# Twenty weight tiles of a two-block kernel: x^T and its remainder as one 512-column operand, sums made by VectorE

## The reference, cut to what matters

```
u = x @ w_in_conv                 # layer 0: query of the cross-attention (256 columns) and 3 x 768 columns
tok = conv(b * c) * c0            # "conv", parts 1, 2 and 0 of u
u = x @ w_in_mlstm                # layer 1: queries and keys of the four heads, 2 x 768 columns
q, k = silu(depthwise_conv4(u_q)), silu(depthwise_conv4(u_k))
a, gate = split(x @ w_in_2[:, 512:1536])
z = a * sigmoid(gate)             # GLU, then a depthwise convolution of 31 taps
```

## Time and profile before

| | |
|---|---|
| median of 3 runs | 1468.51 us (1465.85 to 1469.38) |
| the profiled execution, its own time | 1467.67 us |
| its span, first to last instruction | 1465.9 us |
| PE (TensorE matmul) busy | 1431.2 us, 98% |
| VectorE / ScalarE busy | 905.6 us, 62% / 697.5 us, 48% |
| mean granted clock of TensorE | 0.99 |
| the chain that ended last, PE's share | 88% |

### The profile page before, as it was taken

One profiled execution on the slowest core, in us unless ns is written; L12 is line 12 of the kernel. 1 busy time (PEld: TensorE's weight loads), 2 busy tenths in 40 slices (PEclk: granted clock), 3 DMA queues, 4 the chain that ended last, 5 costly groups with the idle time before them and its releaser, 6 DMA issues.

```text
span 1465.9 us, 21137 instructions
## 1 busy us (share of the span) xinstructions
PE 1431.2 (98%) x8624; PEld 1176.9 (80%) x8624; DVE 905.6 (62%) x1477; ACT 697.5 (48%) x1145; POOL 51.7 (4%) x116
## 2 busy tenths in 40 slices
PE   8999999999999999999999999998999999999995
PEld 7888899888888988889898888888899996445431
DVE  7666577666676765667768666668888685121122
ACT  7455554454554644545755545445546553112211
POOL 0000000000000000000022000001000040000000
PEclk9999999999999999999999999999999999999997
DMA  9754554565555555444345655543554479999996
GB/s 347 282 192 175 199 201 144 201 230 175 199 182 191 202 197 205 173 163 168 131 151 208 251 186 187 200 163 137 181 177 143 144 307 373 391 421 421 421 421 267
DMA packets 49623, 333.80 MB, mean 228 GB/s; under 512 B 5744, under 2 KB 6000, under 8 KB 11632
## 3 DMA queue, kind: packets, MB, share of 16 engines
q1 hardware_dynamic: 47792, 321.50, 58.7%
q10 hardware_dynamic: 1728, 10.88, 1.9%
HBM read 331.31 MB, written 1.05 MB: 227 GB/s over the span
## 4 chain that ended last, share of the span: by engine, by line
PE 88%; DVE 4%; DMA 3%; ACT 2%; POOL 2%; issue 1%; DVEq 0%; SPq 0%; POOLq 0%; ACTq 0%
PE psw L601 55%; PE psy L601 31%; PE psw L604 2%; DMA raw<-in_we 2%; DVE wlo L1912 1%; DMA hold<-in_we 1%; ACT whi L1358 0%; POOL r L2765 0%; DVE x L1997 0%; DVE xs L1921 0%; DVE x L2010 0%; DMA ar<-in_xT 0%; ACT gb L1471 0%; DVE r L1979 0%; POOL rstd L2723 0%
## 5 line engine op out<-in xcount | busy, mean ns | idle before, releaser
L601 PE MATMUL psw<-xs,whi 128*128 128x512 f32 (+1 forms) x2384 | 652.8, 347 | 6.7 <-DVE wlo L1912 6.6
L1912 DVE TENSOR_TENSOR wlo<-raw,whi 128x1024 fp32r<-128x1024 f32 (+4 forms) x415 | 477.0, 1193 | 82.9 <-ACT whi L1358 78.1
L601 PE MATMUL psw<-xs,wlo 128*128 128x256 f32 x1848 | 489.5, 281 | 0.0
L601 PEld LDWEIGHTS psw<-xs,whi 128*128 128x128 f32 x2384 | 404.5, 190 | 54.3 <-DVE wlo L1912 6.6
L1358 ACT ACTIVATE whi<-raw 128x1024 fp32r<-128x1024 f32 (+4 forms) x415 | 402.2, 1024 | 8.7 <-PE psy L601 6.6
L601 PEld LDWEIGHTS psw<-xs,wlo 128*128 128x128 f32 x1848 | 350.4, 190 | 15.2 <-DVE wlo L1912 0.2
L1358 ACT ACTIVATE hf<-psw 128x256 f32<-128x256 f32 x82 | 30.9, 383 | 203.3 <-PE psw L601 203.3
L1950 DVE TENSOR_TENSOR hf<-hf,psw 128x256 f32<-128x256 f32 x82 | 34.0, 419 | 146.3 <-ACT hf L1358 146.3
L1358 ACT ACTIVATE ar<-psw 128x256 f32<-128x256 f32 (+3 forms) x125 | 55.0, 443 | 128.2 <-PE psw L601 115.8
L601 PE MATMUL psy<-whi,hhi 128*128 128x512 f32 x352 | 111.2, 390 | 0.0
L601 PE MATMUL psy<-whi,hlo 128*128 128x512 f32 x352 | 111.0, 389 | 0.0
(11 more groups left out here) (341 smaller groups left out, 1752.2 us busy)
## 6 DMA issues: line engine op xcount, KB each, us to landing
raw<-in_ws SPq DMA_DIRECT2D x189, 1024.0 KB, 4.8
hold<-in_we SPq DMA_DIRECT2D x46, 1024.0 KB, 12.5
raw<-in_we SPq DMA_DIRECT2D x24, 1024.0 KB, 12.9
ar<-in_we SPq DMA_DIRECT2D x21, 1024.0 KB, 13.3
gb<-in_ln ACTq DMA_DIRECT2D x8, 1024.0 KB, 5.0
raw<-in_ws SPq DMA_DIRECT2D x9, 768.0 KB, 4.1
raw<-in_ws SPq DMA_DIRECT2D x4, 672.0 KB, 3.8
raw<-in_ws SPq DMA_DIRECT2D x8, 256.0 KB, 6.7
```

The source lines that it names most:

```text
L601: return e.matmul(o, l, rr, start=start, stop=stop)
L1912: e.tensor_tensor(wlo[i % NS][:, c0:c1], raw_t[slot[i]][:, c0:c1], whi[i % NS][:, c0:c1].bitcast(f32), ALU.subtract).then_inc(*made.up((i, ...
```

## The change

The 20 tiles go through `parted` instead of `pair`. Each now takes two banks. ScalarE copies columns 256 to 511 of each bank to SBUF (`second_halves`), VectorE adds columns 0 to 255 there and thereby empties the bank (`summed`). What read a bank before now reads the sum in SBUF: `cz` is `cb * c2`, `cacc` is multiplied by `c0`, tap 3 and the other taps are made from `zp`, the sigmoid from `sg`, and the GLU's product takes `sg0`. `c2` and `c0` are new tiles in SBUF; the score matmuls of layer 0 wait for VectorE's sum and not for ScalarE's copy.

```
-        cb = arena.take(2 * T)
+        cb, c2, c0 = [blocks(arena.take(2 * T), 256) for _ in range(3)]
...
-        sg = hfl[:, 0:512]
+        sg, sg0 = hfl[:, 0:512], hfl[:, 512:1024]
... tensor
-                need.wait_ge(*act.at("query", l))
+                need.wait_ge(*(act.at("query", 1) if l else dve.at("summed", "q", 0, 1)))
...
-                pair(("q", 0), Tile("w_in_conv", 2304), xhi, xlo, x_rows(1))
+                parted(("q", 0), Tile("w_in_conv", 2304), x_rows(1))
...
-                        pair(("conv", part, j), Tile("w_in_conv", 768 * part + 256 * j), xhi, xlo, x_rows(1))
+                        parted(("conv", part, j), Tile("w_in_conv", 768 * part + 256 * j), x_rows(1))
...
-                        pair(("head", j, part), Tile("w_in_mlstm", 768 * part + 256 * j), xhi, xlo, x_rows(4))
+                        parted(("head", j, part), Tile("w_in_mlstm", 768 * part + 256 * j), x_rows(4))
...
-                pair(("glu", 0, j), Tile("w_in_2", 512 + 256 * j), xhi, xlo, x_rows(6))
+                parted(("glu", 0, j), Tile("w_in_2", 512 + 256 * j), x_rows(6))
... scalar
+            def second_halves(o, *key):
+                for j in range(2):
+                    need.wait_ge(*pe.at("bank", (*key, j)))
+                    copy(o[:, j, :], place[(*key, j)][:, 256:512]).then_inc(*act.up(("half", *key, j)))
... scalar, conv_mixer
-                    from_bank(("conv", 1, j), cb, flat, ("cb", j))
+                    second_halves(cb, "conv", 1, j)
                     steps.pop(0)()
                     w.tile()
+                    second_halves(c2, "conv", 2, j)
                     steps.pop(0)()
                     w.tile()
+                    second_halves(c0, "conv", 0, j)
... scalar, head
-                    copy(zp[part][:, :, 3:259], blocks(b[:, :], 256)).then_inc(*act.up(("zp", j, part)))
+                    second_halves(zp[part][:, :, 3:259], "head", j, part)
...
-                        ins = copy(q_[:, f, :], b[:, 256 * f:256 * f + 256], scale=qwt[:, blk, 3:4])
+                        need.wait_ge(*dve.at("summed", "head", j, part, f))
+                        copy(q_[:, f, :], zp[part][:, f, 3:259], scale=qwt[:, blk, 3:4]).then_inc(*act.up(("tap3", j, part, f)))
... scalar, glu
                 w.tile()
+                need.wait_ge(*(dve.at("zc", 0) if j else act.at("squares", 1, 1)))
+                second_halves(blocks(sg0, 256), "glu", 0, j)
                 between()
                 w.tile()
-                e.activation(sg, place["glu", 1, j][:, :], ACT.Sigmoid).then_inc(*act.up(("sg", j), took(("glu", 1, j))))
+                second_halves(blocks(sg, 256), "glu", 1, j)
+                need.wait_ge(*dve.at("summed", "glu", 1, j, 1))
+                e.activation(sg, sg, ACT.Sigmoid).then_inc(*act.up(("sg", j)))
... vector
+            def summed(o, *key):
+                for j in range(2):
+                    need.wait_ge(*act.at("half", *key, j))
+                    e.tensor_tensor(o[:, j, :], o[:, j, :], place[(*key, j)][:, 0:256], ALU.add).then_inc(
+                        *dve.up(("summed", *key, j), took((*key, j))))
... vector, conv_mixer
                     w.tile()
-                    need.wait_ge(*act.at("cb", j))
-                    need.wait_ge(*pe.at("bank", ("conv", 2, j)))
-                    then(e.tensor_tensor(cz[q][:, :, 2:258], blocks(cb, 256), blocks(place["conv", 2, j][:, :], 256), ALU.mult),
-                         took(("conv", 2, j)))
+                    summed(c2, "conv", 2, j)
+                    need.wait_ge(*dve.at("summed", "conv", 2, j, 1))
+                    then(e.tensor_tensor(cz[q][:, :, 2:258], cb, c2, ALU.mult))
... vector, head
                     need.wait_ge(*pool.at("zp", part))
+                    summed(zp[part][:, :, 3:259], "head", j, part)
... vector, GLU: the sums stand right behind w.tile()
             w.tile()
+            summed(blocks(sg, 256), "glu", 1, 0)
             glu(0)
             w.tile()
+            summed(blocks(sg0, 256), "glu", 0, 1)
             conv_some(5)
             w.tile()
+            summed(blocks(sg, 256), "glu", 1, 1)
             conv_some(5)
```

More of the change, by code:

```diff
@@ L967, in glu @@
             def glu(j, between=lambda: None):
-                pair(("glu", 0, j), Tile("w_in_2", 512 + 256 * j), xhi, xlo, x_rows(6))
+                parted(("glu", 0, j), Tile("w_in_2", 512 + 256 * j), x_rows(6))
                 between()
-                pair(("glu", 1, j), Tile("w_in_2", 1024 + 256 * j), xhi, xlo, x_rows(6))
+                parted(("glu", 1, j), Tile("w_in_2", 1024 + 256 * j), x_rows(6))
             def latents_turned():
@@ L1464, in query @@
                 w.tile()
-                from_bank(("q", l), mem_of[l].qT.rearrange("p b n -> p (b n)"), flat, ("query", l))
+                if l:
+                    from_bank(("q", l), mem_of[l].qT.rearrange("p b n -> p (b n)"), flat, ("query", l))
+                else:
+                    second_halves(mem_of[l].qT, "q", l)
             def score(l, h):
@@ L1522, in head @@
                 def head(j, part):
-                    b = place["head", j, part]
                     q_ = qk[j % 2][part]
-                    need.wait_ge(*pe.at("bank", ("head", j, part)))
                     if j:
                         need.wait_ge(*dve.at("taps", j - 1, part))
-                    copy(zp[part][:, :, 3:259], blocks(b[:, :], 256)).then_inc(*act.up(("zp", j, part)))
+                    second_halves(zp[part][:, :, 3:259], "head", j, part)
                     if j > 1:
@@ L1533, in head @@
                         blk = 6 * part + 2 * j + f
-                        ins = copy(q_[:, f, :], b[:, 256 * f:256 * f + 256], scale=qwt[:, blk, 3:4])
-                        ins.then_inc(*act.up(("tap3", j, part, f), *([took(("head", j, part))] if f else [])))
+                        need.wait_ge(*dve.at("summed", "head", j, part, f))
+                        copy(q_[:, f, :], zp[part][:, f, 3:259], scale=qwt[:, blk, 3:4]).then_inc(*act.up(("tap3", j, part, f)))
                 def head_silu(j, part):
@@ L2107, in conv_mixer @@
                     w.tile()
+                    summed(cb, "conv", 1, j)
                     steps.pop(0)()
                     w.tile()
-                    need.wait_ge(*act.at("cb", j))
-                    need.wait_ge(*pe.at("bank", ("conv", 2, j)))
-                    then(e.tensor_tensor(cz[q][:, :, 2:258], blocks(cb, 256), blocks(place["conv", 2, j][:, :], 256), ALU.mult),
-                         took(("conv", 2, j)))
+                    summed(c2, "conv", 2, j)
+                    need.wait_ge(*dve.at("summed", "conv", 2, j, 1))
+                    then(e.tensor_tensor(cz[q][:, :, 2:258], cb, c2, ALU.mult))
                     steps.pop(0)()
@@ L2126, in conv_mixer @@
                     w.tile()
-                    need.wait_ge(*dve.at("cacc", j, 1))
-                    need.wait_ge(*pe.at("bank", ("conv", 0, j)))
-                    e.tensor_tensor(cacc[q], cacc[q], blocks(place["conv", 0, j][:, :], 256),
-                                    ALU.mult).then_inc(*dve.up(("gated", j), took(("conv", 0, j))))
+                    summed(c0, "conv", 0, j)
+                    need.wait_ge(*dve.at("summed", "conv", 0, j, 1))
+                    e.tensor_tensor(cacc[q], cacc[q], c0, ALU.mult).then_inc(*dve.up(("gated", j)))
                     steps.pop(0)()
@@ L2301, in glu @@
                 need.wait_ge(*act.at("sg", j))
-                need.wait_ge(*pe.at("bank", ("glu", 0, j)))
+                need.wait_ge(*dve.at("summed", "glu", 0, j, 1))
                 need.wait_ge(*pool.at("zc"))
-                e.tensor_tensor(zc[:, 2 * j:2 * j + 2, 30:286], blocks(sg, 256), blocks(place["glu", 0, j][:, :], 256),
-                                ALU.mult).then_inc(*dve.up(("zc", j), took(("glu", 0, j))))
+                e.tensor_tensor(zc[:, 2 * j:2 * j + 2, 30:286], blocks(sg, 256), blocks(sg0, 256), ALU.mult).then_inc(*dve.up(("zc", j)))
             w.tile()
+            summed(blocks(sg0, 256), "glu", 0, 0)
             for n, blks in enumerate(LATENT_BANKS):
@@ L2731, in gpsimd @@
                 rstd_of(1, t)
-            need.wait_ge(*act.at("query", 0))
+            need.wait_ge(*act.at("half", "q", 0, 1))
             for q in range(2):
```

4 lines of the change are left out of this document (1 added, 3 removed).

## The result

The changed kernel takes 1470.38 us (median of 20 runs, 1468.66 to 1471.51) against 1467.32 us for the kernel before beside it (20 runs): a ratio of 1.0019, interval 1.0013 to 1.0025. By that ratio it is 2.8 us more (the medians themselves lie 3.06 us apart), where the forecast had 1.0 us less. The time lies inside the range and inside 0.3%, but it is clear of no change, and on the other side of it. The profiled span grew from 1465.9 to 1469.4 us. In a later round one execution of 2877.62 us (fifth_b) and one of 1773.76 us (the kernel before) are slow ones, left out of the ratios.

What follows compares the result with a forecast made beforehand. It took TensorE to bound the kernel (busy 1431 of 1466 us). Convolution -1.6, head stage +1.2 and GLU -0.64 gave -1.0 us, so 1467.5 us on the median (chance 0.57), range 1464.0 to 1471.5 us.

Steps and rivals of the forecast that it cites:

- The tile: Each of 20 tiles: 32 matmuls in 5.59 us instead of 48 in 5.75, 0.16 us gained, 3.2 us in all.
- Convolution stage: Ten tiles, no wait of PE for a bank, 1.6 us gained.
- The margins: Convolution stage: VectorE's sums empty banks 0.3 and 0.5 us before PE wants them; if both fail, 1 us is given back.
- GLU stage: Four tiles, no wait, 0.64 us gained; first product into `zc` about 1.6 us later.
- Head stage: Six tiles: 0.96 us gained, 1.3 + 0.8 + 0.1 us lost, so 1.2 us slower.
- The two waits for sums: Head stage: PE waits for banks 1.3 us at tile (1,0)'s second half and 0.8 us at (1,1)'s start.
- Attention 2: End of the head stage: two adds lengthen the last tile's copy, taps and SiLU by 0.1 to 0.3 us; costed at 0.1.
- The gain: Head stage: six tiles, each 0.16 us shorter on TensorE, 0.96 us in all.
- A: Rival: no wait in the head stage, as VectorE and ScalarE are further ahead; -3.2 us, 1465.3 us; chance 0.20.
- D: Rival: new tiles miss the feed-forward's pace, nothing gained, the waits stay; +2.2 us, 1470.7 us; chance 0.04.
- C: Rival: ScalarE's and VectorE's chain paces the head stage, 1.3 us at each of six tiles; +4.6 us, 1473.1 us; chance 0.07.
- B: Rival: each of two head-stage waits brings a fall of TensorE's clock, 1.67 us each; +2.3 us, 1470.8 us; chance 0.12.

Runs made afterwards that it cites:

- fifth_b: Changed kernel with the second halves of head tiles (1,0) and (2,0) in the fifth bank, 7, instead of the rotation of four; ratio to the kernel before 1.0014.
- heads_only: Kernel before with only the six head tiles on the new form; ratio to the kernel before 1.0033.
- after_again: The changed kernel run once more, nothing altered, for a second profile; ratio to the kernel before 1.0017.
- taps_first: Changed kernel with ScalarE's and VectorE's next-weight work moved behind each head tile's copies, sums and taps (last tile: behind its SiLU too); ratio to the kernel before 1.0000.
- tap_dve: Changed kernel with the heads' tap 3 made by VectorE from the sum instead of by ScalarE; ratio to the kernel before 1.0014.
- tap_again: Second run, for another profile, of the changed kernel with the heads' tap 3 on VectorE; ratio to the kernel before 1.0014.

## Why the prediction was wrong, by its own steps

**The tile: right.** 32 matmuls and 5.59 to 5.60 us; 8304 matmuls in all.

**Convolution stage: right.** -1.51, -1.65, -1.75 and -1.78 us where -1.6 was forecast, with no wait. The margins held as walked: VectorE's second remainder ends at 233.6 us, and the same stretch begins 0.46 us later than in the kernel before, so that this is 233.1 us against the forecast 233.0 to 233.3; the sum follows at once.

**GLU stage: right.** -0.64 to -0.69 us, forecast -0.64; the first product into `zc` begins 8.01 us after the start of the stage's second tile (1024.27 us in the chain) in place of 6.43 (1020.16), 1.6 us later as said.

**Head stage: the step that failed.** The term of the sum that was mis-sized is its +1.2 us: the two profiles of the changed kernel give +4.5 and +3.3, heads_only +2.95. The two waits for sums were right. The losses at the two ends of the stage were put at 0.1 us, the gain of 0.96 us was taken in full, and a further fall of the clock was left to a rival. In its parts:
- The two waits for banks were walked rightly, 1.42 and 0.91 us against 1.3 and 0.8, at the places named.
- The decay weights' wait was not looked at. It was 0.24 us before, and grew to 0.59 with the new convolution (TensorE comes 0.35 us earlier), 0.43 with the new head tiles (0.19), 0.80 with both (0.56): what TensorE gains ahead of it is waited away, as ScalarE's copies of v come when they come. So 0.4 us of the convolution's gain never reached the stage.
- Attention 2 was costed at 0.1 us "to 0.3" and took 0.64 more. The walk added two sums to the chain from tile to SiLU, and left out that they stand behind VectorE's remainder (until 757.96 us in the changed kernel, 0.9 us after the tile's end) and that ScalarE waits 0.70 us for them; 4.8 us became 5.4.
- The gain was 0.62 us in the stage, not 0.96 (after_again): tile (1,0) with its wait taken off is 0.1 us longer than before. Besides, a gap of 0.4 us more lies ahead of (2,0).
- One additional fall of the clock in one of the two profiles. Tile (1,1) takes 1.56 us more by it, the stage 1.2 us, as the gap ahead of (2,0) goes.

Together, for after_again: 1.4 + 0.9 + 0.55 + 0.63 + 0.4 + 0.1 for a slower attention 0 - 0.62 = 3.3 us, the measured difference.

**The rivals.** A is out, and so is D, as the tiles run at 5.59 us. C had the mechanism that the runs bore out, that the chain of ScalarE and VectorE sets the stage's length: fifth_b showed it by moving the waits, and taps_first by removing them. It was priced at 7.8 us by charging each of six tiles, and given 0.07; the small matmuls of the stage hold it to 2 to 3 us. Its condition, ScalarE's round with the waits in it, was met for a time: the roundings in the changed kernel begin at 722.83, 730.22 and 737.66 us, 7.4 us apart, although ScalarE is busy for only two thirds of the stage. In the first of these rounds 2.9 us are waits for VectorE (1.27 and 1.66 us). What counts is the time from a tile's end to its last sum and its SiLU. B had the price of a fall right (1.67 us, now 1.7), and its 1470.8 us, like D's 1470.7, lies next to the measured 1470.38. For D that is luck, for B in part: B has a fall behind each of the two waits, and the first profile shows one behind the second wait, the second profile none. B alone is not what made the kernel slower, as after_again and heads_only have 3.5 to 4 us of waits and one fall, as many as the kernel before; but the further fall is a part of the loss in the first profile.

Over whole executions the granted clock is 0.990 in the changed kernel (median of 31) and 0.992 in the kernel before (median of 110), some 2.9 us of clock more lost. It is no price: it takes in the end of the span, where the profiles lose 3.4 to 6.9 us from 1425 to 1455 us, and the kernels with the new convolution and GLU alone have 0.991 and are not slower. It leans towards further falls in the executions without a profile, and does not settle it.

The Trainium skill ("TensorE: Matmul & The Clock Gate", section A second HAM failure mode: psum-queue depth-cycling) names short idling between bank groups as what makes the clock swing. The count of falls leans that way, two against one on the mean, and so does their place behind waits; but tap_dve has two falls with no wait for a bank, and the same waits come with and without a fall. Why the one execution has more of them than the other is open.

**The sum.** Its sign hung on one term: three terms of -1.6, +1.2 and -0.6 us, of which the second was 2.1 to 3.3 us too small. With +3.3 in its place the three come to +1.0 us, which turns the sign but is not the measured +2.8. The first profile has the remainder in the further fall and in 0.5 us between 800 and 1016 us, the second in 1.7 us behind 1210 us. Which of these a usual execution has is not shown.

## What to carry to other kernels

When the emptying of a bank goes from one engine to two, walk the whole way from a tile's end to the release and to the tile's last consumer, with everything that stands in line on both queues, and put the copy, the sum and what follows ahead of the work for later tiles; here that order alone took the ratio from 1.0019 to 1.0000 (with what it changed in waits and falls of the clock together), and a further bank gave nothing that can be told from the error (1.0014). A gain ahead of a wait is worth only the part that the wait doesn't take back, so list the small waits too (0.2 us can become 0.8). A wait that covers another (the decay weights over the banks of (0,0)) has to be priced before it is moved.

## What the runs showed of the hardware

TensorE's clock loses time in equal portions: in 18 profiles the loss between 680 and 800 us was 1.7, 3.4, 5.1 or 6.8 us (to 0.05), with the granted clock at 0.50 in each fall. It differs by one portion between two executions of one kernel (changed kernel with the same waits: 3.4 and 1.7; tap_dve and tap_again: 3.4 and 5.1). The time up to 188.7 us, ahead of every edit, differs by 1.4 us between executions of one kernel, half of what this change cost. It is not the clock: the granted clock is 1.00 in every slice of 5 us up to 680 us, in all 18 profiles.
